# The last three eighths of an output projection in upper and lower parts, and who splits the weights

## What is computed

```
heads = concat(rms_norm(y_pool), rms_norm(y_attn), rms_norm(y_ssm))
h = layer_norm(DN_ALPHA * x + heads @ w_out[i], ln1_g[i], ln1_b[i])
combine = route(h, w_router, router_bias)
ffn = moe(h, combine, w_exp_gate[i], w_exp_up[i], w_exp_down[i])
ple = sigmoid(h @ w_ple_gate[i]) * (p[i] @ w_ple_proj[i])
x = layer_norm(DN_ALPHA * h + ffn + ple, ln2_g[i], ln2_b[i])
```

## Time and profile before

| | us |
|---|---|
| median of 3 runs | 431.24 (431.01 to 431.34) |
| the profiled execution | 431.64 |
| its span in the trace | 429.9 |
| PE busy | 411.6 (96% of the span) |
| DVE busy | 256.0 (60%) |
| ACT busy | 128.4 (30%) |
| POOL busy | 93.2 (22%) |

### The profile page before, as it was taken

One profiled execution on the slowest core, in us unless ns is written; L12 is line 12 of the kernel. 1 busy time (PEld: TensorE's weight loads), 2 busy tenths in 40 slices (PEclk: granted clock), 3 DMA queues, 4 the chain that ended last, 5 costly groups with the idle time before them and its releaser, 6 DMA issues.

```text
span 429.9 us, 5587 instructions
## 1 busy us (share of the span) xinstructions
PE 411.6 (96%) x2163; PEld 237.5 (55%) x2163; DVE 256.0 (60%) x468; ACT 128.4 (30%) x231; POOL 93.2 (22%) x132
## 2 busy tenths in 40 slices
PE   8899999999999999999999999999999999999980
PEld 4677655469666556676587876333333333333360
DVE  2999975986873989998778423111110112225887
ACT  4722335025497890210721011011111011111332
POOL 3830279274001700000000641011111111000000
PEclk9999999999999999999999999999999999999996
DMA  8993104251997992011571329999999999959113
GB/s 278 431 390 115 49 2 70 62 130 73 267 410 276 294 372 88 29 49 50 204 335 48 149 60 352 426 412 422 419 409 422 419 408 417 423 212 319 72 49 146
DMA packets 33626, 102.76 MB, mean 239 GB/s; under 512 B 14882, under 2 KB 16082, under 8 KB 26816
## 3 DMA queue, kind: packets, MB, share of 16 engines
q1 hardware_dynamic: 26032, 92.79, 56.1%
q0 software_dynamic: 4016, 7.97, 5.6%
q10 hardware_dynamic: 3552, 1.65, 1.4%
HBM read 93.29 MB, written 15.24 MB: 252 GB/s over the span
## 4 chain that ended last, share of the span: by engine, by line
PE 66%; issue 23%; DVE 4%; DMA 3%; POOL 1%; ACT 1%; DVEq 0%; POOLq 0%; ACTq 0%
PE bank L1301 20%; PE bank L1311 10%; PE bank L946 6%; PE bank L994 5%; PE bank L1296 3%; PE bank L961 3%; PE bank L986 3%; PE bank L1003 2%; PE bank L982 2%; PE bank L1061 2%; PE bank L1051 2%; POOL slot_scratch L595 1%; PE bank L989 1%; PE bank L1117 1%; PE bank L1116 1%
## 5 line engine op out<-in xcount | busy, mean ns | idle before, releaser
L1301 PE MATMUL bank<-region_a,region_g 128*64 128x512 f32 (+1 forms) x224 | 77.8, 594 | 0.0
L1311 PE MATMUL bank<-region_a,region_c 128*64 128x512 f32 (+1 forms) x160 | 43.8, 596 | 0.0
L1877 DVE TENSOR_TENSOR region_c<-region_c,bank 128x256 f32<-128x256 f32 x12 | 5.0, 421 | 64.7 <-ACT region_c L907 64.7
L1301 PE MATMUL bank<-region_h,region_g 128*64 128x512 f32 (+1 forms) x96 | 42.4, 594 | 0.0
L1301 PE MATMUL bank<-region_b,region_g 128*64 128x512 f32 (+1 forms) x96 | 42.4, 594 | 0.0
L1301 PE MATMUL bank<-region_c,region_g 128*32 128x512 f32 (+1 forms) x96 | 42.4, 594 | 0.0
L1870 DVE COPY region_g<-bank 128x512 f32<-128x512 f32 x24 | 15.5, 685 | 40.8 <-PE bank L1296 40.8
L1301 PEld LDWEIGHTS bank<-region_a,region_g 128*64 128x64 f32 (+1 forms) x224 | 22.2, 123 | 25.1 <-issue 24.4
L1145 PE MATMUL bank<-region_b,region_e 128*128 128x512 f32 x68 | 32.9, 607 | 0.0
L907 ACT ACTIVATE region_c<-bank 128x256 f32<-128x256 f32 x12 | 4.6, 383 | 83.9 <-PE bank L1301 83.9
L946 PE MATMUL bank<-region_e,region_a 128*128 128x512 f32 x64 | 28.0, 595 | 0.0
(11 more groups left out here) (360 smaller groups left out, 877.4 us busy)
## 6 DMA issues: line engine op xcount, KB each, us to landing
region_a<-in_w_exp_down SPq DMA_DIRECT2D x10, 1024.0 KB, 11.2
region_a<-in_w_exp_gate SPq DMA_DIRECT2D x7, 1024.0 KB, 7.9
region_a<-in_w_exp_up SPq DMA_DIRECT2D x7, 1024.0 KB, 11.5
region_b<-in_w_out SPq DMA_DIRECT2D x1, 4096.0 KB, 15.6
expert_scratch<-zero_scratch SPq DMA_DIRECT2D x8, 512.0 KB, 10.0
region_c<-in_w_ple_gate SPq DMA_DIRECT2D x2, 1536.0 KB, 23.6
region_b<-in_w_exp_gate SPq DMA_DIRECT2D x3, 1024.0 KB
region_b<-in_w_exp_up SPq DMA_DIRECT2D x3, 1024.0 KB
```

Of the source, the lines that this page charges most:

```text
L1301: return mm(out_[at:at + width].rearrange("p (u n) -> p u n", u=2), x[:, k, at:at + width], w[:, k], start=(k == 0), stop=(k == KD - 1), t ...
L1311: return mm(bank[banks[half]][at:at + width, :], act_e[:, r, 2, k * P + at:k * P + at + width], w[:, k, half * 512:half * 512 + 512], star ...
```

## The change

1. `WO_SPLIT` gets slices 2, 3 and 4. So `out_proj` does all three groups by `mix_split`, and no plain matmul is left in tiles 1 to 3.
2. ACT copies three more slices of heads and three more of weights. The new upper parts lie where the second half of `pg_hi` and the ramp `t_iota` will be written.
3. The lower parts of weights 2, 3 and 4 are made by GpSimd, in place over `w_o`, half by half: six subtractions of 128x512, the first three after tile 0 has read the first half. TensorE waits for them (`wo_lo_two`) in tile 1. GpSimd's ramp comes after the whole projection.
4. ACT's copies of the gate's slices 4 to 7 wait until the projection is over: 4 and 5 ahead of the router's copy, 6 and 7 behind its sigmoid. DVE subtracts 3 (between tiles 0 and 1), 4 and 5 (ahead of the router's choice). GpSimd subtracts 6 and 7 (128x1024 each).
5. One semaphore is saved: `y_back` is counted on `y_out`.

```diff
-WO_SPLIT = (5, 6, 7, 0, 1)
+WO_SPLIT = (5, 6, 7, 0, 1, 2, 3, 4)
-PG_FIRST, PG_ORDER = (0, 1, 2), (5, 6, 7, 4, 3)
+PG_FIRST, PG_LAST = (0, 1, 2), (4, 5, 6, 7)
...
             add_squares(4, 2, 0)
+            for half in range(2):
+                cols = slice(half * 512, half * 512 + 512)
+                gp.wait_ge(S["wo_hi_set"], 16)
+                gp.wait_ge(S["pe_wo"], half + 1)
+                for k in (2, 3, 4):
+                    g.tensor_tensor(wo_lo[k][:, cols], w_o[:, k, cols], wo_hi[k][:, cols], ALU.subtract).then_inc(S["wo_lo_two"], 1)
+            gp.wait_ge(S["pe_wo"], 2 * NT)
             link(g.iota(t_iota, pattern=[[1, T]], base=0, channel_multiplier=0, allow_small_or_imprecise_dtypes=True))
 
+
+            for k in PG_LAST[2:]:
+                gp.wait_ge(S["ple_hi_set"], 1 + NT + k - 3)
+                g.tensor_tensor(pg_lo[:, k * D:(k + 1) * D], pg_part[:, k, :], pg_hi[:, k * D:(k + 1) * D],
+                                ALU.subtract).then_inc(S["wo_lo_two"], 1)
...
-            for k in PG_ORDER[:4]:
-                gate_upper(k)
...
-            gate_upper(PG_ORDER[4])
+            gate_upper(3)
...
             hidden_upper(3)
+            gate_upper(4)
+            gate_upper(5)
...
             a.activation(r_s, bank[B_COUNT][:, 0:NT * NE], ACT.Sigmoid).then_inc(S["sig_rt"], 1)
-            ac.wait_ge(S["ple_lo_set"], KD + NT)
+            gate_upper(6)
+            gate_upper(7)
+            ac.wait_ge(S["ple_lo_set"], 4 + NT)
...
                         mix_split(t, half, group)
-                    mix_part(t, half, 2).then_inc(S["pe_wo"], 1)
+                    if t == 1:
+                        pe.wait_ge(S["wo_hi_set"], 16)
+                        pe.wait_ge(S["wo_lo_two"], 3 * half + 3)
+                    mix_split(t, half, 2).then_inc(S["pe_wo"], 1)
...
                 if t == 0:
-                    gate_lower_of(1)
-                    gate_lower_of(2)
+                    dv.wait_ge(S["ple_hi_set"], 1)
+                    gate_lower(3)
                 elif t == 1:
-                    gate_lower_of(3)
                     hidden_lower(0)
-                elif t == 2:
-                    gate_lower_of(4)
...
             hidden_lower(3)
+            for k in PG_LAST[:2]:
+                dv.wait_ge(S["ple_hi_set"], 1 + NT + k - 3)
+                gate_lower(k)
```

More of the change, by code:

```diff
@@ L820, in _ @@
             for k in WO_SPLIT:
+                if k == 2:
+                    ac.wait_ge(S["pv_evac"], 3)
                 a.activation(hd_hi[k][:], hdT[:, k, P:T], ACT.Copy).then_inc(S["wo_hi_set"], 1)
             ac.wait_ge(S["wo_in"], 16)
-            for k in (0, 1, 5, 6, 7):
+            for k in (0, 1, 5, 6, 7, 2, 3, 4):
                 a.activation(wo_hi[k][:], w_o[:, k, :], ACT.Copy).then_inc(S["wo_hi_set"], 1)
@@ L1155, in mix_split @@
                 for i, (x, w) in enumerate(terms):
-                    mm(bank[WO_AT[half][group]][:], x[:, (t - 1) * P:t * P], w[:, half * 512:half * 512 + 512],
-                       start=(i == 0), stop=(i == len(terms) - 1))
+                    last = mm(bank[WO_AT[half][group]][:], x[:, (t - 1) * P:t * P], w[:, half * 512:half * 512 + 512],
+                              start=(i == 0), stop=(i == len(terms) - 1))
+                return last
             def sum_squares(group, t):
@@ L1199, in out_proj @@
                         if t == 1 and half == 0:
-                            pe.wait_ge(S["wo_hi_set"], (7, 10)[group])
-                            pe.wait_ge(S["wo_lo_set"], (7, 10)[group])
+                            pe.wait_ge(S["wo_hi_set"], (10, 13)[group])
+                            pe.wait_ge(S["wo_lo_set"], (10, 13)[group])
                         mix_split(t, half, group)
-                    mix_part(t, half, 2).then_inc(S["pe_wo"], 1)
+                    if t == 1:
+                        pe.wait_ge(S["wo_hi_set"], 16)
+                        pe.wait_ge(S["wo_lo_two"], 3 * half + 3)
+                    mix_split(t, half, 2).then_inc(S["pe_wo"], 1)
             def turn_h(t):
@@ L1224, in ple_gate @@
                 if half == 0:
-                    pe.wait_ge(S["ple_lo_set"], KD + t + 1)
+                    pe.wait_ge(S["ple_lo_set"], 4 + t + 1)
+                elif t == 0:
+                    pe.wait_ge(S["ple_lo_set"], 4 + NT + 2)
+                    pe.wait_ge(S["wo_lo_two"], 8)
                 for c in range(KD):
@@ L1243, in ple_proj @@
                     if k == NT:
-                        pe.wait_ge(S["ple_hi_set"], len(PG_ORDER) + NT + 2)
-                        pe.wait_ge(S["ple_lo_set"], KD + NT + 2)
+                        pe.wait_ge(S["ple_hi_set"], 1 + NT + 4 + 2)
+                        pe.wait_ge(S["ple_lo_set"], 4 + NT + 4)
                     terms = [(x[:, c * T + t * P:c * T + t * P + P], w[:, c * D + half * 512:c * D + half * 512 + 512])
@@ L1640, in _ @@
             row_max(5)
-            dv.wait_ge(S["y_back"], 48)
+            dv.wait_ge(S["y_out"], 96)
             for m in range(3):
@@ L1682, in _ @@
             dv.wait_ge(S["pe_mix"], 1)
-            out_lower(0, 6)
-            out_lower(1, 7)
-            gate_lower_of(0)
+            out_lower(0, 9)
+            out_lower(1, 10)
             dv.wait_ge(S["pe_mix"], 2)
-            out_lower(5, 8)
-            out_lower(6, 9)
-            out_lower(7, 10)
+            out_lower(5, 11)
+            out_lower(6, 12)
+            out_lower(7, 13)
             dv.wait_ge(S["rms_sqrt"], 3)
```

21 lines of the change are left out of this document (10 added, 11 removed).

## The result

| | us |
|---|---|
| before, median of 4 runs | 431.24 (431.01 to 431.34) |
| changed, median of 4 runs | 434.59 (434.43 to 436.38) |
| ratio | 1.0087, 95% interval 1.0065 to 1.011 |
| the profiled execution of the changed kernel | 436.38, span 434.5 |

The changed kernel is slower, by 3.35 us. Forecast were 431.4 and the range 428.8 to 433.0: the prediction is wrong. The profiled execution is 1.8 us longer than the other three (434.43, 434.53, 434.65), so its rows show one thing that those may not have; the experiments tell which.

A forecast was written before the change was run, and what follows sets the result against it. Between projection and experts, TensorE (by work) and the router's chain (by latency) bound it, ending within 0.6 us of each other. Terms: -3.1 + 4.3 - 1.1 = +0.1 us, so 431.4 us on the median; range 428.8 to 433.0.

The forecast's parts named there:

- TensorE's saving: Projection, tiles 1 to 3: nine fp32r matmuls replace three plain ones, 0.52 us less per half, six halves, 3.1 us less.
- ScalarE ahead of tile 1: Copies ahead of the norm's square roots: queue grows by nothing, eighth weight copy near 157.8, wanted at 166.26; cost nothing.
- VectorE ahead of tile 1: Three more head subtractions against one gate subtraction less: 0.3 us cost against 0.33 cover; nothing, or some tenths.
- GpSimd's first six: Weight subtractions of 128x512 at 1.27 us, ending at 167.7; waits in tile 1 cost nothing up to 2.0 us each.
- the cover of 0.2 us in tile 2: Start of tile 2: DVE has read the first banks at 174.4, TensorE would start at 174.6; covered by 0.2 us.
- The gate's slices 4 and 5: Ahead of the router's choice: ACT copies 0.1 us late, DVE subtractions (2.35) fit into 3.30 us idle; cost nothing.
- The gate's slices 6 and 7: Beside the router's choice: two GpSimd subtractions stop DVE's instructions, 4.3 us longer; bounds 3.4 and 4.8.
- The sum: Router to end: TensorE stands still 2.7 us, saving given back; -3.1 + 4.3 - 1.1 = +0.1 us, 431.4 on the median.
- The rivals: Four cases: no hold of small DVE instructions (12%), shorter hold (12%), dearer GpSimd (8%), TensorE waiting for GpSimd in tile 1.
- Rival (c): GpSimd subtractions cost more: at 1.5 times the price up to +6, 437 us, 8%; with milder forms 18% for over 0.9 slower.
- (b): Router's choice: hold shorter or half hidden; at 1.5 us per subtraction the sum is -1.4, about 430.0; 12%.

The follow-up runs named there:

- e1: Changed kernel, with ScalarE loading the square root's table ahead of its waits for the gate's weights and the sum of squares: 432.24 us, ratio 1.0027.
- e5: Changed kernel with the edits of e1 and e4 together: table loaded ahead of the waits, no GpSimd instruction beside the router's choice: 427.83 us, ratio 0.9923.
- e6: Kernel before, with a second, already fulfilled wait ahead of ScalarE's square roots, so the table load carries the wait for the sum of squares: 434.08 us, ratio 1.006.
- e4: Changed kernel, but GpSimd subtracts the gate's slices 6 and 7 ahead of the router's choice, not beside it; table load stays late: 429.58 us, ratio 0.9973.
- e9: Changed kernel with the edits of e1 and e3 together: table loaded ahead of the waits, ten useless matmuls in TensorE's router wait: 431.10 us, ratio 0.9999.
- e3: Changed kernel with ten useless matmuls on TensorE while it waits for the router's choice: 432.53 us, ratio 1.0044.
- e2: Changed kernel with seven useless matmuls on TensorE in its wait ahead of tile 1; table load stays late: 433.41 us, ratio 1.0056.
- e7: Kernel before, with four GpSimd subtractions of 128x512 from the router's sigmoid on, and the ramp rewritten behind them: 433.89 us, ratio 1.007.

## Why the prediction was wrong, by its own steps

- **TensorE's saving, 3.1 us.** Right: 2.05 us per group; from the start of tile 1 to the turn of t = 2 the kernel before took 37.92 us and e1 34.62, 3.3 less; 3.25 less at the end in e5.
- **ScalarE ahead of tile 1, "cost nothing".** The first step that failed. It compared the lengths of the copies that come and go, which was right (three of weights and three shorter ones of heads more, four of the gate less; the queue was over at 157.61 against 157.33), and asked only whether the weight parts come in time. It didn't ask what the copies that go had been doing for the waits around them: they took up the wait for `wpg_in`, and kept the table load ahead of the wait for `pe_sq`. The load, 1.28 us, fell behind it: 1.3 us on the start of tile 1. e6 shows it alone.
- **VectorE ahead of tile 1, GpSimd's first six, the cover of 0.2 us in tile 2.** Right in all: VectorE had 0.39 us of idle time ahead of its last weight parts against 0.33 before, and the six took 1.27 us each. They were over at 166.84 and not at 167.7, so the norm's scaling lost nothing where 0.45 us was allowed. Tile 2 came right behind tile 1 in e1 and e5 (turns of t = 0 and 1 11.80 us apart).
- **The gate's slices 4 and 5.** Right: the router's copy at 212.95 against 213.35, nothing lost.
- **The gate's slices 6 and 7, 4.3 us.** Right: 4.2 measured, and e4 takes them back to 8.88 us of choice.
- **The sum, "TensorE stands still for 2.7 us: the saving is given back there".** The second step that failed. The idle time came as forecast (2.49), but it was priced at its own length, so that it would cost nothing beyond the saving. What it did to the clock behind it was left out. Of the 1.6 to 3.0 us that TensorE lost by that, the 0.6 of the earlier trace rows (TensorE waiting for the gather) are cover; the rest, 1.0 to 2.4, reaches the end, now by TensorE and no longer by the gather.
- **The rivals.** All four were about GpSimd's price. Rival (c), slower, was the right sign with the wrong cause: no GpSimd row was over 1.3 us for 512 columns. In (b) there is a slip: at 1.5 us per subtraction the terms give -1.2 (-3.1 + 3.0 - 1.1), not -1.4; its 430.0 stands. None asked what an idle time does, though the forecast itself made one of 2.7 us where the trace of before had none over 0.61 in that part.

How the medians add up, from e9's 431.1 (the sum as forecast): the late table load adds some 1.3 (e3's four shorter executions, 432.1 to 432.6, against e9: 1.0 to 1.5); the half clock at the router 1.1 in its short form (e1) and some 2.4 in its long form (e2's longer executions, 434.7, against e3's 432.3); the half clock in tile 1 adds 1.6 where it falls. All with the long form give 431.1 + 1.3 + 2.4 + 1.6 = 436.4, the profiled execution of 436.38. The other three, at 434.5, are 2.1 above what the table load explains. They can have the long form at the router and none in tile 1 (434.8), or the short form and tile 1 (431.1 + 1.3 + 1.1 + 1.6 = 435.1). Both lie somewhat above the measured 434.5; their mean clock (0.983) doesn't tell, and they have no rows. That stays open. It changes nothing in the two causes.

## What to carry to other kernels

When a change takes instructions from between two waits of an engine, look at which instruction now carries which wait, and above all at a table load, which stands in no line of the code: load the table by hand ahead of the waits. When a sum ends in "this engine now stands still for x us", x is not the price: on TensorE idle times of 1.9 to 2.5 us cost up to 1.6 and up to 3.0 us on top here, and to fill them even with matmuls of no use was worth 1.2 to 2.3 us. And a GpSimd instruction that reads SBUF doesn't belong beside a chain of small instructions of VectorE: one of 16 columns waited out the whole of it.

## What the runs showed that was not expected

- The same idle time of TensorE has no fixed price. 0.6 us and 1.37 us drew no half clock in the profiled executions; 1.84 none in one (e7); 1.94 drew it in two profiled executions of five, and by the times in 5 of 12 executions of e4; 2.5 in three of three. A kernel with such an idle time has two groups of times, and a single profiled execution may belong to either: the expectation for e4 went wrong by reading one.
- The stretch behind it is not of one length either: 1.6, 2.9 and 3.0 us were lost behind the same 2.5 us.
- A wait that was long fulfilled, placed ahead of another, cost 3.0 us of 431 (e6), though it never held anything up.
- GpSimd's 4.8 us in two pieces held VectorE's choice for 4.2 us, 4.4 us in four pieces and the ramp's 0.56 behind them for 3.5 (e7). Even the ramp, which reads no tile, held a copy: 0.62 us in place of 0.20.
